# Second query tile projected at the start of the mixing; new order of the vector engine's work between the two attentions

## What is computed

```python
def _project_in(u, w_in):
    z = u @ w_in
    q, k, v, f, g_a, g_b = jnp.split(z, cuts, axis=-1)
    return _heads(q) * ATTN_SCALE, _heads(k), _heads(v), f, g_a, g_b

def _merge_branches(f, o_na, g_a, g_b, w_fourier, w_na_out, w_out):
    branch_a = _fourier_mix(f) @ w_fourier
    branch_b = _merge_heads(o_na) @ w_na_out
    return (jax.nn.sigmoid(g_a) * branch_a + jax.nn.sigmoid(g_b) * branch_b) @ w_out
...
        y_s = _ffn_sublayer(y_s, m_lat, 0, w_ff1_up[l], w_ff1_down[l], ln_g[l], ln_b[l])
        q, k, v, f, g_a, g_b = _project_in(_modulate(y_s, m_lat, 1), w_in[l])
        o = _neighbourhood_attention(q, k, v, cache_k[:, l], cache_v[:, l], rpb[l])
        mix = _merge_branches(f, o, g_a, g_b, w_fourier[l], w_na_out[l], w_out[l])
        y_s = _post_norm(y_s, mix, m_lat, 1, 1.0, ln_g[l], ln_b[l])
```

## Time and profile before

| | us |
|---|---|
| time, median of 3 runs | 2670.79 (2670.07 to 2671.3) |
| the profiled execution's own time | 2670.52 |
| its span, first to last instruction | 2668.7 |
| PE busy (matmul) | 2622.8, 98% |
| DVE busy | 2065.9, 77% |
| ACT busy | 1059.1, 40% |
| mean granted TensorE clock | 0.993 of full |

### The profile page before, as it was taken

The page is one execution under the profiler, slowest core; times in us unless marked ns, Lnnn a source line. Parts: engine busy times, 40 slices in busy tenths (PEclk is TensorE's granted clock), DMA queues, the critical chain, the costliest instruction groups (busy, mean ns, idle before and its releaser), DMA issues.

```text
span 2668.7 us, 46216 instructions
## 1 busy us (share of the span) xinstructions
PE 2622.8 (98%) x18014; PEld 2593.3 (97%) x18014; DVE 2065.9 (77%) x3919; ACT 1059.1 (40%) x1866; POOL 0.2 (0%) x4
## 2 busy tenths in 40 slices
PE   8999999899999999999999999999999999999998
PEld 8999999899999999999999999998999999999997
DVE  7787986767756888798689878786776568988877
ACT  5145253533222534525352534535242225253453
POOL 0000000000000000000000000000000000000000
PEclk9999999999999999999999999999999999999998
DMA  7433422222333232242223243221413322324321
GB/s 279 138 110 110 160 95 95 92 86 96 123 126 112 78 111 95 93 160 95 95 95 119 87 153 111 98 96 60 145 61 130 126 79 95 119 87 153 105 101 59
DMA packets 77804, 295.38 MB, mean 111 GB/s; under 512 B 25168, under 2 KB 31568, under 8 KB 54096
## 3 DMA queue, kind: packets, MB, share of 16 engines
q1 hardware_dynamic: 51552, 211.16, 22.2%
q10 hardware_dynamic: 26096, 82.16, 8.9%
HBM read 289.62 MB, written 6.82 MB: 111 GB/s over the span
## 4 chain that ended last, share of the span: by engine, by line
PE 95%; DVE 3%; DMA 1%; ACT 1%; issue 1%; ACTq 0%; SPq 0%; DVEq 0%
PE psum L787 10%; PE psum L792 10%; PE psum L791 10%; PE psum L527 6%; PE psum L529 6%; PE psum L530 6%; PE psum L572 4%; PE psum L575 4%; PE psum L576 4%; PE psum L1053 3%; PE psum L1055 3%; PE psum L1056 3%; PE psum L676 2%; PE psum L680 2%; PE psum L681 2%; PE psum L888 2%
## 5 line engine op out<-in xcount | busy, mean ns | idle before, releaser
L792 PE MATMUL psum<-Th,w_lo 128*128 128x320 f32 x1024 | 316.4, 309 | 0.0
L787 PE MATMUL psum<-Th,w_hi 128*128 128x320 f32 x1024 | 316.3, 309 | 0.0
L791 PE MATMUL psum<-Tl,w_hi 128*128 128x320 f32 x1024 | 316.1, 309 | 0.0
L1114 ACT ACTIVATE w_hi<-w_raw 128x2048 fp32r<-128x2048 f32 x98 | 187.4, 1912 | 311.2 <-DVE acc L1675 157.0
L527 PE MATMUL psum<-Hh,w_hi 128*128 128x320 f32 x896 | 277.7, 310 | 2.8 <-DVE Hl L1979 2.4
L529 PE MATMUL psum<-Hl,w_hi 128*128 128x320 f32 x896 | 277.2, 309 | 0.0
L530 PE MATMUL psum<-Hh,w_lo 128*128 128x320 f32 x896 | 277.1, 309 | 0.0
L1592 DVE TENSOR_TENSOR w_lo<-w_raw,w_hi 128x2048 fp32r<-128x2048 f32 x98 | 224.2, 2288 | 53.5 <-ACT w_hi L1114 52.9
L787 PE MATMUL psum<-Uh,w_hi 128*128 128x320 f32 x768 | 237.5, 309 | 0.0
L791 PE MATMUL psum<-Ul,w_hi 128*128 128x320 f32 x768 | 237.2, 309 | 0.0
L792 PE MATMUL psum<-Uh,w_lo 128*128 128x320 f32 x768 | 236.6, 308 | 0.0
(11 more groups left out here) (326 smaller groups left out, 7253.4 us busy)
## 6 DMA issues: line engine op xcount, KB each, us to landing
w_raw<-in_wstream SPq DMA_DIRECT2D x184, 1024.0 KB, 4.8
ada_w<-in_ada ACTq DMA_DIRECT2D x145, 512.0 KB, 3.4
first_w<-in_ada SPq DMA_DIRECT2D x9, 512.0 KB, 14.8
first_w<-in_ada_first SPq DMA_DIRECT2D x6, 512.0 KB, 9.0
gath<-in_rpb SPq DMA_DIRECT2D x128, 24.0 KB, 3.5
G<-gath ACTq DMA_DIRECT2D x4, 768.0 KB, 4.6
X<-in_xT SPq DMA_DIRECT2D x8, 320.0 KB, 15.4
yT<-X SPq DMA_DIRECT2D x8, 192.0 KB, 1.9
```

Source lines behind the costliest of these rows:

```text
L787: m1 = pe.matmul(out, hi[:, k, :], rh, start=(start and k == 0), stop=False, skip_group_check=not start)
L791: pe.matmul(out, hi[:, k, :], rl, start=False, stop=False, skip_group_check=not start)
L792: mm = pe.matmul(out, lo[:, k, :], rh, start=False, stop=(k == 3), skip_group_check=not start)
L1114: act.activation(hi, w_raw[:, r, :, :], ACT.Copy).then_inc(s_whi, 1)
```

## The change

Each layer's second query tile (queries of heads 4 to 7) is moved in the weight stream from behind the first attention to the place behind the first value tile. It is rounded into a buffer of its own (`query_hi`) and split into two pieces (`query_lo`), since no single free area is large enough. Its products with half 0 run between the value blocks and `both(tiles, 1)`: first all 32 matmuls that need only the high part of the weights, with the variance's sum after the eighth, then the 16 that need the low part. Its products with half 1 run behind `both(tiles, 1)`. The queries are stored in columns of `Otok` that the second attention writes later, and are read from there. Between the attentions only the key tile (96 matmuls) and the values are left. The two value blocks at the start share one PSUM use, and the clearing of `bm` moves behind the query copies. ACT issues the loads for the first attention behind the root instead of ahead of it. One pair of conditioning chunks moves ahead of the first attention; between the attentions DVE does the low part of the value tile and a pair of chunks before it copies the first keys.

The core of the diff:

```diff
         spare_h = spare("spare_h", 61440, 81920)
-        spare_v = spare("spare_v", 66048, 76288)
+        spare_v = spare("spare_v", 59392, 77952)
+        query_hi = at("query_hi", 51200, [P, 16, P], F32R)
+        query_lo = (at("query_lo0", 86144, [P, 12, P], F32R), at("query_lo1", 31232, [P, 4, P], F32R))
...
+            def later_query(h, low_ready, begun=0, between=None):
+                u = next_use()
+                rh, rl = [[x[:, k, h * HT:(h + 1) * HT] for k in range(KD)] for x in (Uh, Ul)]
+                for b in range(2):
+                    for k in range(KD):
+                        out = bank(u, b, 0, HT)
+                        m1 = pe.matmul(out, query_hi[:, b * KD + k, :], rh[k], start=(k == 0), stop=False,
+                                       skip_group_check=True)
+                        if begun and (b, k) == (0, 0):
+                            started(m1, begun)
+                        pe.matmul(out, query_hi[:, b * KD + k, :], rl[k], start=False, stop=False,
+                                  skip_group_check=True)
+                        if between is not None and (b, k) == (0, 3):
+                            between()
+                low_ready()
+                for b in range(2):
+                    for k in range(KD):
+                        mm = pe.matmul(bank(u, b, 0, HT), query_low(b * KD + k), rh[k], start=False,
+                                       stop=(k == KD - 1), skip_group_check=True)
+                filled(mm)
...  the matmul engine, mixing
                 v_tile = take(spare_v)
-                for t in range(2):
-                    token_use(t, v_tile)
-                variance_of(un)
+                first_values(v_tile)
+                query_tile = tile.at()
+                tile.next()
+                pe.wait_ge(s_whi, query_tile)
+                later_query(0, lambda: pe.wait_ge(s_wsplit, query_tile), between=lambda: variance_of(un))
                 both(tiles, 1, None)
                 C["u"].next(2 * KD)
+                later_query(1, lambda: None, 3)
                 for t in range(2, T // P):
-                    token_use(t, v_tile, 2 if t == 2 else 0)
+                    token_use(t, v_tile)
                 attention(0)
                 tiles = Tiles()
-                for m in range(4):
-                    if m == 2:
-                        attention_stored()
+                for m in range(2):
...  the scalar engine, mixing
                 round_tile(1, spare_v)
+                round_tile(2, (query_hi, None))
                 squares(1)
...
+                deviation(use_no[0], 1)
                 attention_inputs(l, 0)
-                deviation(use_no[0], 1)
...
                 round_tile()
+                ada_pair()
                 for t in range(2, 5):
                     value_copies(t)
                 store_context(l, 0)
                 attention()
 
                 round_tile()
+                ada_pair()
+                ada_pair()
                 act.wait_ge(s_free, use.at(-1))
                 attention_inputs(l, 1)
-                skip(4)
+                skip(2)
+                round_tile()
                 ada_pair()
-                round_tile()
-                for _ in range(3):
-                    ada_pair()
-                round_tile()
...  the vector engine, mixing
                 low_tile(spare_v)
-                link(dve.memset(bm[:, :, 256:384], 0.0))
                 for m, dst in enumerate((qT, kT)):
                     rows(dst, 0, -ATTN_SCALE if m == 0 else 1.0)
                 centre(use_no[0], 1)
+                low_query()
-                normalise(1, {3: [lambda: value(0)], 5: [lambda: value(1)]})
+                normalise(1, {3: [lambda: value(0, True)], 5: [lambda: value(1, True)]})
+                later_query_rows(0)
...
                 low_tile()
+                gate_pair(0)
+                later_query_rows(1)
+                link(dve.memset(bm[:, :, 256:384], 0.0))
...
                         low_tile()
-                        for m in range(4):
-                            if m == 2:
-                                low_tile()
+                        gate_pair(1)
+                        for m in range(2):
...
+                            if m == 0:
+                                gate_pair(2)
+                        low_tile()
+                        gate_pair(3)
                         for t in range(5):
-                            if t == 1:
-                                low_tile()
                             value(t)
```

More of the change, by code:

```diff
@@ L865, in attention @@
                                 po = HD * e
-                                pe.matmul(scores(e, 256), qT[po:po + HD, hp, j * P:(j + 1) * P],
+                                pe.matmul(scores(e, 256), query(hh, po, hp, j),
                                           kT[po:po + HD, hp, KEY0[j] * ROWS:KEY0[j] * ROWS + 256], start=True, stop=True)
@@ L869, in attention @@
                                 po = HD * e
-                                pe.matmul(psum[:, e, 256:384], qT[po:po + HD, hp, j * P:(j + 1) * P],
+                                pe.matmul(psum[:, e, 256:384], query(hh, po, hp, j),
                                           ckT[po:po + HD, 2 * hh + hp, :], start=True, stop=True).then_inc(s_sc, 1)
@@ L874, in attention @@
                                 po = HD * e
-                                pe.matmul(scores(e, P), qT[po:po + HD, hp, LAT:T], kT[po:po + HD, hp, LAT:T],
+                                pe.matmul(scores(e, P), query(hh, po, hp, QB), kT[po:po + HD, hp, LAT:T],
                                           start=True, stop=True).then_inc(s_sc, 1)
@@ L1473, in attention, with value_copies @@
                 use_no[0] += -use_no[0] % 4
-            def value_copies(t):
-                act.wait_ge(s_full, C["full"].next())
+            def value_copies(t, paired=False):
+                b = t if paired else 0
+                if b == 0:
+                    act.wait_ge(s_full, C["full"].next())
                 if t < 3:
-                    i = act.activation(V[0:64, 4 + t, :], bank(use_no[0], 0, 0, 256, 64, 128), ACT.Copy)
+                    i = act.activation(V[0:64, 4 + t, :], bank(use_no[0], b, 0, 256, 64, 128), ACT.Copy)
                 if 0 < t < 4:
-                    i = act.activation(V[64:128, 3 + t, :], bank(use_no[0], 0, 0, 256, 0, 64), ACT.Copy)
+                    i = act.activation(V[64:128, 3 + t, :], bank(use_no[0], b, 0, 256, 0, 64), ACT.Copy)
                 if t < 4:
@@ L1483, in value_copies @@
                     C["func"].next()
-                use.next()
-                use_no[0] += 1
+                if (t, paired) != (0, True):
+                    use.next()
+                    use_no[0] += 1
             def attention_inputs(l, hh):
@@ L2268, in rows, with later_query_rows, low_query, value @@
                 free(i)
[L2270 removed]
+            def later_query_rows(h):
                 dve.wait_ge(s_full, C["full"].next())
+                for b in range(2):
+                    cols = slice(256 + b * P, 256 + (b + 1) * P)
+                    whole, part_, j0, lo, c0 = ((0, 256), (256, HT), 0, 256 + b * P, 2) if h == 0 else \
+                        ((64, HT), (0, 64), 3, 256 + b * P + 64, 2)
+                    dve.tensor_scalar(Otok[:, j0:j0 + 2, cols],
+                                      bank(use_no[0], b, *whole).rearrange("p (j n) -> p j n", j=2), -ATTN_SCALE, None,
+                                      ALU.mult)
+                    i = dve.tensor_scalar(Otok[:, c0, lo:lo + 64], bank(use_no[0], b, *part_), -ATTN_SCALE, None,
+                                          ALU.mult)
+                free(i)
+            def low_query():
+                r = raw_slot[0]
+                raw_slot[0] ^= 1
+                dve.wait_ge(s_whi, C["whi"].next())
+                dve.tensor_tensor(query_lo[1][:, :, :], w_raw[:, r, 12:16, :], query_hi[:, 12:16, :].bitcast(F32),
+                                  ALU.subtract)
+                dve.tensor_tensor(query_lo[0][:, :, :], w_raw[:, r, 0:12, :], query_hi[:, 0:12, :].bitcast(F32),
+                                  ALU.subtract).then_inc(s_wsplit, 1)
+            def value(t, paired=False):
+                b = t if paired else 0
+                if b == 0:
+                    dve.wait_ge(s_full, C["full"].next())
                 if t < 4:
                     dve.wait_ge(s_func, C["func"].next())
[L2274 removed]
+                i = dve.tensor_copy(V[:, t if t < 4 else 7, :], bank(use_no[0], b, 0, 256))
+                if (t, paired) != (0, True):
+                    free(i)
             def mixing(l):
+                def gate_pair(m):
+                    ada_pair(mods[1], 2 * KD + 2 * m, loads(l, C["ada"].n - l * (3 * ADA_SUB), 0))
                 low_tile(spare_v)
[L2278 removed]
                 for m, dst in enumerate((qT, kT)):
@@ L2410, in weight_stream @@
         for hh in range(2):
```

(4 more changed lines are left out.)

31 lines of the change are left out of this document (22 added, 9 removed).

## The result

The changed kernel takes 2652.62 us (median of 4 runs, 2651.79 to 2653.52); the kernel before, run beside it, 2670.43 us (4 runs, 2666.69 to 2671.3). The ratio is 0.9938, interval 0.9926 to 0.995: **faster by 0.6%**, and 0.4 us from the forecast of 2653.0. The medians are 17.8 us apart. The profiled execution took 2653.52 us, its span is 2651.7 us where it was 2668.7.

The account below looks back on a forecast made before the run. PE bounds the kernel, through idle waits and the slow clock behind them. Layer one -8.87 us (+5.82 - 14.08 - 0.61), layer two -9.20, together -18.1 from 2670.52: median 2652.7, taken as 2653; range 2650.5 to 2660.5.

Parts of the forecast that it names:

- PE at the start: Start of mixing: moved matmuls, 7.04 us a half, fill PE's wait; 0.12 us idle left before the variance's sum.
- DVE at the start: Ahead of the reciprocal: two subtractions add 2.28 us, 1.67 covered by the wait for the root; 0.61 us delays half 1.
- Rival 2: Start of half 1: DVE's delay not covered, 2.28 us instead of 0.61; 1.67 us a layer, 2656; chance 0.07.
- Half 1: Half-1 matmuls: start at 503.44 after 0.43 us wait, take 14.08 us at full clock, DVE keeping up by 0.3 us.
- rival 1: Half-1 matmuls: clock falls all the same after two short pauses; 4.0 us of losses stay, 2657; chance 0.08.
- Work moved to hidden places: Before the first attention: query copies, `bm` and the chunk pair end about 529, PE arrives 533.2; costed at nothing.
- Between the attentions: PE loses 96 matmuls, 14.08 us, and a 0.61 us value-copy wait; DVE just fast enough, 0.9 us to spare.
- I take no stall: Chunk loads between the attentions: no DVE stall assumed, 0 to 4.62 us a pair kept for the range.
- Rival 3: Between the attentions: one 4.62 us load stall a layer makes DVE hold PE 3.7 us a layer; 2660; chance 0.12.
- the chain of 24.7 us: DVE between the attentions: first value block copied 24.7 us after PE's first matmul; PE needs its banks at 25.6.
- Rivals 4 and 5: 4: all three pairs stall, 2683, chance 0.03; 5: query tile not there in time, PE idle as before, about 2669, 0.03.
- rival 4: Between the attentions: three 4.62 us stalls, DVE chain 38.6 us, PE waits 13.0 us; slower, 2683; chance 0.03.

Follow-up runs that it names:

- experiment with the doubled low part: Kernel after with the query tile's 1536-column subtraction on DVE issued a second time ahead of half 1; 2656.14 us, ratio to before 0.9952.
- the run with a pair put back: Kernel after with the pair of chunks moved ahead of the first attention put back between the attentions; 2667.39 us, ratio to before 0.9996.
- the kernel before with fillers: Kernel before with six dead matmuls in the last steps of each attention; 2669.59 us, ratio to before 1.0001.
- query tile behind half 1: Kernel after with all 96 second-query-tile matmuls behind the half-1 matmuls, so nothing covers the wait; 2670.09 us, ratio to before 1.0005.

## Why the prediction was right

**The bound.** It was PE's idle time and the clock behind it. Filling the wait with matmuls of no use took the clock loss away, uncovering it in the new kernel brought back everything. One reading was wrong, without harm to the sum: "everything else on PE's list is below a microsecond at a time". The earlier trace rows leave out longer waits in the feed-forwards and at the start, which the view of PE's waits of the kernel before has and the change doesn't touch:

```profile
PE psum L725 <- DMA first_w<-in_ada_first: 7.9, 3, 5.7
PE psum L603 <- DVE last_sq L1870: 2.4, 1, 2.4
PE psum L527 <- DVE Hl L1979: 2.4, 1, 2.4
...
PE psum L734 <- DVE Ul L2065: 1.3, 1, 1.3
```

**PE at the start.** The first half-1 matmul was predicted at 503.44; with the 0.80 us that the profile after is ahead of the one before, that is 502.64, and it started at 502.63. Nothing had to be waited for at the variance's sum. The wait of 0.43 us came out as a pause of 0.3 us. From the mean's sum to attention 1 the stretch grew by 5.95 and 5.63 us; predicted were 5.82, and 0.33 less (5.49) in layer two.

**DVE at the start.** The delay of 0.61 us was 0.60. Rival 2 (2.28) is out, since the reciprocal stands right behind the subtractions. The experiment with the doubled low part shows that the next 1.7 us in each layer would have cost 1.8 us in one and 3.3 in the other.

**Half 1.** 14.08 us predicted, 14.15 measured, at full clock: rival 1 is out.

**Work moved to hidden places.** The query copies, `bm` and the pair of chunks were costed at nothing, and attention 1 shows no wait for them.

**Between the attentions.** Predicted 14.69 us less, measured 14.42 and 13.93. The step that was a little off is "I take no stall": in layer one a load stalled DVE for 1.04 us, which used up the margin of 0.9 (the stretch is 0.3 us longer than the 28.65 us of kernels where PE shows no wait there); in layer two, for 1.51 us:

```profile
1896.42 1.23 DVE L1726 CUSTOM_DVE_ANT_0 junk<-ada_w,csilu 128x1024 bf16<-128x1024 f32 x1 [1.51 <-DMA ada_w<-in_ada]
...
1910.44 0.39 PE L938 MATMUL psum<-w_hi,Uh 128*128 128x256 f32 x1 [0.57 <-DVE V L2353]
```

Both lines are of the kernel after, the second from PE's timeline. Rival 3 had the right mechanism, but 4.62 us was the stall of the old order. Its count of what DVE loses there is short: besides a pair and a low part it is two blocks of query rows, four copies, and not one; the chain of 24.7 us has it right. Rivals 4 and 5 are out with the result; the chain that rival 4 describes is what the run with a pair put back shows, at a wait of 5.8 us instead of 13.0. The sum without the odd drops is -8.47 and -8.30, -16.8 us, against -18.1 predicted: 1.0 us of the difference lies between the attentions and 0.3 at the start.

**What agreed by luck.** The terms, as measured, give 16.8 us; the medians differ by 17.8 and the prediction said 18.1. That it came within 0.4 us is therefore in part luck, and the scatter of four runs, 1.7 us for the kernel after and 4.6 for the kernel before, is larger than that. The profiled difference is 17.0 us, and not only these terms are in it. Three that the prediction doesn't have: the kernel before is 0.8 us behind when the mixing starts, most of it by a clock drop at 124 us, in the first feed-forward, which the changed code doesn't touch and which the profile after lacks; at the ends of attentions the kernel after has one drop more (+1.5 us); and in the first attention of layer one a wait of 0.76 us has gone. The trace of the kernel before has it on PE's timeline, and its cause on ACT's, where a store of the new values took 1.46 us to issue:

```profile
532.02 0.62 PE L898 MATMUL psum<-ident,pr 128*128 128x128 f32 x2 [0.76 <-ACT pr L1459]
```

```profile
528.59 1.46 ACTq L1498 DMA_DIRECT2D new_v<-V  x1
...
530.08 1.28 ACT L1459 ACT_TABLE_LOAD   x1 [5.13 <-issue]
```

The same store in the kernel after, on ACT's timeline:

```profile
534.03 0.61 ACTq L1550 DMA_DIRECT2D new_v<-V  x1
```

In layer two of every kernel it takes 0.63 us, and in layer one it is long only in the two kernels where the wait stands (1.69 us and a wait of 0.98 us in the kernel before with fillers). So the wait follows the issue time; why the issue takes longer there was not tested. The prediction had named "a PE wait that I have not listed in the first attention" as what could make it wrong; what it missed was of the other sign.

**The rule weighed.** The Trainium skill, page "TensorE: Matmul & The Clock Gate", section "A second HAM failure mode: psum-queue depth-cycling", says, of a bf16 kernel with 512 columns, that frequent short pauses between groups of matmuls can make the clock swing between its levels. The prediction said that this trace doesn't agree where it can be compared. At the start of the mixing that held: clock 1.00 behind a pause of 0.3 us. But it had looked only there. At the ends of the attentions, pauses of 0.4 and 0.8 us within two microseconds are followed by 0.76 and 0.81 in 4 of 28 cases. There the traces fit the rule, as something that happens now and then; a gain from filling the pauses is not shown.

## What to carry to other kernels

When the matrix engine is the bound and waits once for a long vector chain, look for work on other data that is already loaded and costs the same wherever it stands; its gain is the idle time plus the slow stretch behind it, and it must be checked that the vector engine, whose stretch it leaves, has less to do there as well. The stretch that gets shorter is the place where the next wait arises: here it had 0.9 us of margin, and a load's stall of a microsecond used it up. Where only the clock is to be saved, matmuls without a use in a long wait do it, written to a bank that is about to be overwritten: 36 of them in the 5.4 us wait gave back 1.75 and 2.08 us, of which half was lost again at the next place. Before a drop of the clock that one profile shows is put down to a pause, look for the same pause in every other profile.

## What the hardware showed unexpectedly

- The clock can fall from 1.00 to the level of 0.5 behind pauses far shorter than 5.4 us: behind 1.9 us in one layer and not in the other, and behind 0.4 and 0.8 us close together. At these places a drop cost about 1.5 us.
- It doesn't come every time, though the code and the pause are the same. All nine profiles have a PE wait of 2.4 us in the first feed-forward (`Hl`, at 124 us), which no edit touches. Behind it the clock is low in four (before, before with fillers, query tile behind half 1, low part twice) and full in five. The 150 matmuls that follow take 23.5 to 23.6 us with the drop and 22.8 without. The windows of the kernel before and, below, of the kernel after:

```profile
124.00:128.00 4.00, 3.18 (x12) 3.18 (x13) 3.93 (x6) 1.16 (x1) 0.00 (x0) 0.57 0.35 123
```

```profile
124.00:128.00 4.00, 3.35 (x23) 3.35 (x24) 3.93 (x6) 0.99 (x1) 0.00 (x0) 1.00 0.32 110
```

- The runs of the kernel before spread from 2666.0 to 2671.5 us, and their mean granted clock goes with it. In the 40 runs beside the experiments it is 0.996 in nine, which took 2666.0 to 2667.3 us, and 0.993 or 0.994 in 26, which took 2668.2 to 2671.5. Which drops make the difference can't be told from the mean.
- The issue of one and the same store on ACT took 0.61 to 1.69 us.
